# Values of a three-branch attention layer: turned on TensorE, or by VectorE's 32x32 turns and a trip through DRAM

## What is computed

```python
h = rmsnorm(x, norm_w[layer])
proj = h @ w_in[layer]
# 8 stick-breaking heads, each block of 128 queries against the keys up to its end
z = einsum('bhqd,bhkd->bhqk', qb, kb) * scale
log_fail = where(strict, -softplus(z), 0.0)
a = where(strict, exp(log_sigmoid(z) + suffix_sum(log_fail)), 0.0)
outs.append(einsum('bhqk,bhkd->bhqd', a, vb))
# 8 forgetting heads: causal softmax of q.k/8 + cum[t] - cum[s], then the same product with vb
# 4 memory heads: softmax over 256 memory tokens
y = rmsnorm_per_head(concat(sb_out, fx_out, m_out)) * out_norm_w * silu(gate)
x = x + y @ w_out[layer]
return rmsnorm(x, final_norm_w)
```

## Time and profile before

| | |
|---|---|
| median of 3 runs | 793.46 us (793.13 to 793.98) |
| the profiled execution: its own time | 793.03 us |
| its span, first to last instruction | 791.1 us |
| mean granted TensorE clock | 0.998 of full speed |
| busy: PE, DVE, ACT, POOL | 776.6, 605.0, 445.7, 257.7 us |
| DMA | 37708 packets, 93.25 MB, mean 118 GB/s |

### The profile page before, as it was taken

How to read it: one execution, slowest core, us unless ns; L and a number is a source line. 1 busy time by engine, 2 the same in 40 slices (tenths; PEclk the granted TensorE clock), 3 DMA queues, 4 the chain that set the end, 5 groups by cost and what they waited for, 6 DMA issues and landing times.

```text
span 791.1 us, 11916 instructions
## 1 busy us (share of the span) xinstructions
PE 776.6 (98%) x4030; PEld 653.2 (83%) x4030; DVE 605.0 (76%) x1206; ACT 445.7 (56%) x920; POOL 257.7 (33%) x440
## 2 busy tenths in 40 slices
PE   8999999999999999999999999999999999999997
PEld 8878887888888888888888888888888887878775
DVE  6877687776789777768977777898767688685676
ACT  7767765556646555665745667465555574542232
POOL 1112733242156326223823521383234124210000
PEclk9999999999999999999999999999999999999999
DMA  9413824124113412521261142106213398233523
GB/s 355 134 63 141 278 98 148 54 69 106 67 54 98 144 40 69 134 67 54 65 175 41 68 125 77 54 27 178 76 55 81 110 386 300 82 107 107 187 96 143
DMA packets 37708, 93.25 MB, mean 118 GB/s; under 512 B 5000, under 2 KB 13192, under 8 KB 36624
## 3 DMA queue, kind: packets, MB, share of 16 engines
q1 hardware_dynamic: 37648, 92.50, 36.1%
HBM read 61.91 MB, written 21.66 MB: 106 GB/s over the span
## 4 chain that ended last, share of the span: by engine, by line
PE 85%; DVE 7%; DMA 2%; ACT 2%; issue 2%; SPq 0%; POOL 0%; ACTq 0%; DVEq 0%; POOLq 0%
PE banks L867 16%; PE banks L869 15%; PE banks L868 15%; PE banks L1037 8%; PE banks L912 8%; PE banks L1057 5%; PE banks L1024 4%; PE banks L1056 4%; PE banks L1023 4%; PE banks L1108 1%; DMA hT<-wo_dram 1%; PE banks L984 1%; DMA work<-part_dram 1%; PE banks L1077 1%; DVE pT L1876 1%
## 5 line engine op out<-in xcount | busy, mean ns | idle before, releaser
L867 PE MATMUL banks<-hT,w_parts 128*128 128x512 f32 x576 | 237.6, 412 | 0.3 <-DVE sb_heads L1735 0.2
L869 PE MATMUL banks<-hT,w_parts 128*128 128x512 f32 x576 | 225.8, 392 | 0.0
L868 PE MATMUL banks<-hT,w_parts 128*128 128x512 f32 x576 | 225.4, 391 | 0.0
L1266 ACT ACTIVATE pT<-banks 128x512 fp32r<-128x512 f32 x208 | 92.4, 497 | 126.7 <-PE banks L1037 126.4
L1876 DVE TENSOR_TENSOR pT<-banks,pT 128x512 fp32r<-128x512 f32 x208 | 108.4, 563 | 66.6 <-ACT pT L1266 65.3
L869 PEld LDWEIGHTS banks<-hT,w_parts 128*128 128x128 f32 x576 | 108.1, 188 | 24.5
L867 PEld LDWEIGHTS banks<-hT,w_parts 128*128 128x128 f32 x576 | 108.5, 188 | 15.8 <-DVE sb_heads L1735 1.0
L868 PEld LDWEIGHTS banks<-hT,w_parts 128*128 128x128 f32 x576 | 109.0, 189 | 13.6
L1534 POOL TENSOR_TENSOR w_parts<-w_raw,w_parts 128x1024 fp32r<-128x1024 f32 x34 | 81.4, 2395 | 91.9 <-ACT w_parts L1165 91.9
L1541 POOL TENSOR_SCALAR_AFFINE_SELECT work<-work 128x128 f32<-128x128 f32 x64 | 30.4, 475 | 192.7 <-ACT work L1243 192.7
L1836 DVE TENSOR_TENSOR_SCAN work<-work 128x639 f32<-128x639 f32 (+3 forms) x64 | 90.7, 1418 | 0.7 <-POOL work L1541 0.6
(11 more groups left out here) (258 smaller groups left out, 1355.9 us busy)
## 6 DMA issues: line engine op xcount, KB each, us to landing
w_raw<-in_w_tiles SPq DMA_DIRECT2D x36, 512.0 KB, 3.9
hT<-wo_dram SPq DMA_DIRECT2D x14, 512.0 KB, 8.4
fx_heads<-fx_heads SPq DMA_DIRECT2D x8, 512.0 KB, 7.8
negL<-negL_dram SPq DMA_DIRECT2D x8, 512.0 KB, 6.1
yT_dram<-silu SPq DMA_DIRECT2D x8, 512.0 KB, 4.1
sb_heads<-sb_heads SPq DMA_DIRECT2D x8, 512.0 KB, 6.7
negL<-yT_dram SPq DMA_DIRECT2D x8, 512.0 KB, 4.9
work<-in_x SPq DMA_DIRECT2D x6, 512.0 KB, 6.7
```

The source lines that it names most:

```text
L867: pe.matmul(o, w[0][:, k, :], hT[:, 0, k, tok], start=(k == 0), stop=False)
L868: pe.matmul(o, w[0][:, k, :], hT[:, 1, k, tok], start=False, stop=False)
L869: mm = pe.matmul(o, w[1][:, k, :], hT[:, 0, k, tok], start=False, stop=(k == KT - 1))
L1266: act.activation(pT[:, n % 3, 0, cols], banks[:, T_BANK + n % 2, cols], ACT.Copy).then_inc(t_hi, 1)
```

## The change

The piece of values leaves PSUM by DVE's transpose, which turns each 32x32 block in place and writes it to the same buffer as the copy did. SP stores the buffer with four DMAs to a DRAM tensor in which the blocks stand at their turned places, and fetches it with one DMA, positions on the partitions, into the lower part's place of the value region. ACT copies from there to the upper part, DVE subtracts in place. The small job VT with its PE transposes and its use of the shared bank is gone; its semaphores `vt_hi` and `small_done` are replaced for the values by `v_out`, `v_in`, `v_hi`, `v_done`. The ticks of fetch and split come from a new table: for phases 3 to 9 the split is in ticks 13 and 15 of the phase before (c = 0, 1), for phase 2 in ticks 21 and 25. The load of the forget gates of the second head follows the fetch.

```diff
+def values_ticks():
+
+    out = []
+    for of in range(2, N_PH):
+        for c in range(2):
+            done = READ_TICK[piece_of("V", c, of)] - 1
+            fetch = max(done + 2, UNITS * (of - 1) + 7) if of > 2 else done + 8
+            out.append((of, c, fetch, max(fetch + 3, UNITS * (of - 1) + 13 + 2 * c) if of > 2 else fetch + 3))
+    return out
...
+    v_dram = nc.dram_tensor("v_dram", (N_PH, 2, CW, P), F32, kind="Internal").ap()
...
+        def v_in_rows(of, c):
+
+            return v_of(region_of(of))[:, 4 * c:4 * c + 4, 1:3, :]
...
+                if p.what == "V":
+                    store_values(q)
                 if closes_tile(p) and p.what == "K":
                     copy_keys(p.of, q)
 
+            def store_values(q):
+
+                p = PIECE[q]
+                sp.wait_ge(piece_done, q + 1)
+                rows = v_dram[p.of, p.c, :, :].rearrange("(j k) (i d) -> i k j d", k=Q4, d=Q4)
+                for i in range(P // Q4):
+                    sp.dma_start(rows[i], v_raw(p.of, p.c)[i * Q4:(i + 1) * Q4, :].rearrange("k (j d) -> k j d", d=Q4)).then_inc(v_out[p.c], 16)
+
+            def fetch_values(of, c):
+
+                sp.wait_ge(v_out[c], 64 * (of - 1))
+                if of > 2:
+                    sp.wait_ge(pv_done, STEP0[4 * (of - 1)])
+                else:
+                    for j in (1, 2):
+                        sp.wait_ge(wo_out[j], 32)
+                sp.dma_start(v_in_rows(of, c).bitcast(F32).rearrange("p b x c -> p b (x c)"),
+                             v_dram[of, c, :, :].rearrange("(b p) w -> p b w", p=P)).then_inc(v_in[c], 16)
+                if c == 1 and PHASES[of][0] == "fx":
+                    load_negL(PHASES[of][1], 1)
...
                 for q in DONE[i]:
                     piece_end(q)
+                for of, c, fetch, _ in VALUES:
+                    if i == fetch:
+                        fetch_values(of, c)
...
-                if p.what == "VT":
-                    pe.wait_ge(piece_done, piece_of("V", p.c, p.of) + 1)
-                    for b in range(4):
-                        mm = pe.transpose(o[:, b * P:(b + 1) * P], v_raw(p.of, p.c)[:, b * P:(b + 1) * P], ident[:, :])
...
                 if t.first and t.group % 4 == 0 and x0.kind != "mm":
-                    pe.wait_ge(small_done, small_of("VT", 1, x0.ph) + 1)
+                    pe.wait_ge(v_done, 2 * (x0.ph - 1))
...
+            def values_hi(of, c):
+                act.wait_ge(v_in[c], 16 * (of - 1))
+                act.activation(v_of(region_of(of))[:, 4 * c:4 * c + 4, 0::3, :], v_in_rows(of, c).bitcast(F32), ACT.Copy).then_inc(v_hi, 1)
...
                 if u % UNITS < 2:
 
-                    act.wait_ge(small_ready, READY_BEFORE[small_of("VT", 1, t.ph)] + 1)
+                    for c in range(2):
+                        act.wait_ge(v_out[c], 64 * (t.ph - 1))
...
-                    dve.tensor_copy(v_raw(p.of, p.c), src).then_inc(piece_done, 1)
+                    dve.transpose(v_raw(p.of, p.c), src).then_inc(piece_done, 1)
...
-                elif p.what == "VT":
-                    dve.wait_ge(vt_hi, VT_BEFORE[n] + 1)
-                    d = v_of(region_of(p.of))[:, 4 * p.c:4 * p.c + 4, :, :]
-                    dve.tensor_tensor(d[:, :, 1:3, :], src.rearrange("p (b h c) -> p b h c", b=4, h=2),
-                                      d[:, :, 0::3, :].bitcast(F32), ALU.subtract).then_inc(small_done, 1)
...
+            def values_lo(of, c):
+                dve.wait_ge(v_hi, 2 * (of - 2) + c + 1)
+                v = v_of(region_of(of))[:, 4 * c:4 * c + 4, :, :]
+                dve.tensor_tensor(v[:, :, 1:3, :], v[:, :, 1:3, :].bitcast(F32), v[:, :, 0::3, :].bitcast(F32), ALU.subtract).then_inc(v_done, 1)
```

More of the change, by code:

```diff
@@ L290, in small_pieces @@
             out.append(Small("N3", c, ph - 1, UNITS * ph + N3_AT + N3_LATER.get(ph - 1, 0)))
[L291 to L299, removed]
     for c in (1, 0):
@@ L307 @@
 SMALL_AT = [[n for n, p in enumerate(SMALL) if p.tick == i] for i in range(N_TICKS)]
-READY_BEFORE = firsts(1 if p.what in ("VT", "MT", "NT") else 0 for p in SMALL)
+READY_BEFORE = firsts(1 if p.what in ("MT", "NT") else 0 for p in SMALL)
 NT_BEFORE = firsts(1 if p.what == "NT" else 0 for p in SMALL)
-VT_BEFORE = firsts(1 if p.what in ("VT", "MT") else 0 for p in SMALL)
+MT_BEFORE = firsts(1 if p.what == "MT" else 0 for p in SMALL)
+def values_ticks():
[6 more added lines that the diff above has]
+    return out
+VALUES = values_ticks()
 def next_phase(i, at, later={}):
@@ L977, in small @@
                 p = SMALL[n]
-                if n and p.what in ("VT", "MT", "NT"):
+                if n and p.what in ("MT", "NT"):
                     pe.wait_ge(small_done, n)
                 o = banks[:, SMALL_BANK, :]
-                if p.what == "VT":
-                    pe.wait_ge(piece_done, piece_of("V", p.c, p.of) + 1)
-                    for b in range(4):
-                        mm = pe.transpose(o[:, b * P:(b + 1) * P], v_raw(p.of, p.c)[:, b * P:(b + 1) * P], ident[:, :])
-                elif p.what == "MT":
+                if p.what == "MT":
                     pe.wait_ge(piece_done, piece_of("memV", p.c, None) + 1)
@@ L1207, in split_next, with mem_values_hi @@
                     split_hi(w_follows(PIECE[q].tile))
-            def values_hi(n):
+            def mem_values_hi(n):
                 p = SMALL[n]
                 act.wait_ge(small_ready, READY_BEFORE[n] + 1)
[L1212 to L1224, removed]
+                for b in range(MB):
+                    ins = act.activation(mem_v[:, b, p.c, 0::3, :],
+                                         banks[:, SMALL_BANK, b * P:(b + 1) * P].rearrange("p (h c) -> p h c", h=2), ACT.Copy)
+                ins.then_inc(mt_hi, 1)
+            def values_hi(of, c):
+                act.wait_ge(v_in[c], 16 * (of - 1))
+                act.activation(v_of(region_of(of))[:, 4 * c:4 * c + 4, 0::3, :], v_in_rows(of, c).bitcast(F32), ACT.Copy).then_inc(v_hi, 1)
             def sigmoids(u):
@@ L1442, in _ @@
             for n in range(len(MEM_VALUES_AT)):
-                values_hi(n)
+                mem_values_hi(n)
             evacuate(7)
@@ L1490, in _ @@
                 for n in SMALL_AT[i]:
-                    if SMALL[n].what in ("VT", "MT"):
-                        values_hi(n)
+                    if SMALL[n].what == "MT":
+                        mem_values_hi(n)
                     if SMALL[n].what == "N1" and SMALL[n].of == LAST:
@@ L1496, in _ @@
                         y_end_hi(SMALL[n].of - LAST + 1, SMALL[n].c)
+                for of, c, _, at in VALUES:
+                    if i == at:
+                        values_hi(of, c)
                 for n in SMALL_AT[i + 1] if i + 1 < N_UNITS else []:
@@ L1764, in finish_small @@
                 if p.what == "MT":
-                    dve.wait_ge(vt_hi, VT_BEFORE[n] + 1)
+                    dve.wait_ge(mt_hi, MT_BEFORE[n] + 1)
                     for b in range(MB):
@@ L2082, in _ @@
                     lower_part(n)
+                for of, c, _, at in VALUES:
+                    if i == at:
+                        values_lo(of, c)
                 for n in SMALL_AT[i]:
```

7 lines of the change are left out of this document (2 added, 5 removed).

## The result

Slower by 1%: 801.23 us against 793.72 us for the kernel before on the same chip, ratio 1.010 (95% interval 1.0087 to 1.0112). I had forecast 787.9 us, in a range of 785.6 to 790.9. The profiled execution took 803.15 us (span 801.2), 1.9 us above the median of its runs; against the 793.03 us of the profiled execution before (span 791.1) that is 10.1 us more.

What follows compares the result with a forecast made beforehand. PE's own instruction stream was taken to set the pace nearly everywhere. A PE gain of 6.9 us less 1.3 us of border stalls, other terms 0, gave 5.6 us: from 793.46 to 787.9 us, range 785.6 to 790.9.

Steps and rivals of the forecast that it cites:

- PE's gain: On TensorE: removing four transposes saves 0.43 us per piece of values, 6.9 us for 16 pieces.
- The recorded duration: Rival on PE: each transpose is worth its 272 ns duration, so the time falls to 776 us; chance 0.02.
- The border stalls: Moved copy and subtract delay PE's scores into phases 4 and 6 (0.4 us each) and 9 (0.5): 1.3 us lost.
- The landing: Each piece's stores of 128 B runs to DRAM land after about 8 us, hidden, so costing 0.
- 512 B rule: Trainium skill's rule against small DMA runs: 512 B for full rate, read-modify-write below; kept as a rival.
- factor of 19: Skill's warning on turning by strided plain copy: a 3.9 us landing would become 74, and the time exceed about 945 us.
- DMAs and SP's queue: Four added stores and one fetch per piece, 80 issues on SP, stay hidden before the next weight load: 0 us.
- The stores hold SP: Rival: 40 us landings hold SP's queue, weight loads come 22 us late in seven phases, about 945 us; chance 0.04.
- The subtract waits for POOL: Rival: DVE's subtract waits out POOL's split at seven borders, 12 us less the 6.9 gained: 798.5 us; chance 0.07.

Runs made afterwards that it cites:

- the version with the borders moved: Changed kernel with phase 2's splits at ticks 28 and 36, later phases' splits at 13 and 14 (stick-breaking running) or 12 and 14 (forgetting): 789.39 us, ratio 0.9942.
- the late splits: Changed kernel with phase 2's two splits (ACT's copy, DVE's subtract) at ticks 28 and 36 instead of 21 and 25: 788.93 us, ratio 0.9946 to the kernel before.
- the long-run experiment: Changed kernel with values stored as rows of 2048 B instead of 128 B runs, leaving them in wrong places: 801.46 us, ratio 1.0098 to the kernel before.
- the two profiles: Changed kernel profiled at 803.15 us, then run again unchanged for a second profile; that run took 801.77 us.

## Why the prediction was wrong

The sign was wrong through one step. By the others:

- **PE's gain: right.** 0.43 us a turn from the starts; 0.43 by the ticks (6.1 us for 14 pieces, about 0.8 for the other two). By the Trainium skill ("TensorE: Matmul & The Clock Gate", Part 4), whose figure is for bf16, it would have been 0.275 us for each transpose; four of them gave 0.43, 0.11 each. The recorded duration (272 ns) agrees with the page and is not a price on a full PE.
- **The border stalls: right** in place and size at three (0.4, 0.4, 0.5 us), and undone one by one in the version with the borders moved. Smaller losses of 0.1 to 0.3 us at ticks 49, 92 and 124 I had not counted. With the late splits the whole came to 4.7 us less than before, where my sum was 5.6.
- **The landing: wrong and harmless.** I scaled 3.9 us by the number of runs to 8; it is 2.6 to 3.2. The Trainium skill's 512 B rule ("DMA: Bandwidth & Descriptors", Specifications) agrees in direction with the 0.5 to 0.6 us a store of the long-run experiment. Its factor of 19 ("VectorE: DVE Perf Modes", The three transpose paths) compares with the hardware's DMA transpose, which no run here used; no store of the changed kernel came near the 74 us that I had worked out from it (the longest landed after 5.2).
- **"DMAs and SP's queue": the step that failed.** It ended "At 8 us after about 241 they land near 249, before the next weight load is due at 250.8. So I take 0." Phase 3 stood for all phases, and what I asked was whether the new stores would delay SP's old work. The harm went the other way: SP's old work delayed the new fetch. For phases 3 to 9 the fetches are ordered at tick 7 or 8 of the phase before, six to eight ticks ahead of the copy; for phase 2 at ticks 18 and 22, three ahead, on a queue that is busy with w_out until 104 and then stands for POOL until 123.9 (119.5 in the kernel before, where it could be read). I wrote "(for phase 2: 21 and 25)" and never held these ticks against the earlier trace rows's counterpart in phase 1. The term was 0 and should have been 13 to 14 us: 9.0 to 10.6 in the two stops at the scores, the rest the reduced clock and slowed work around them.
- **The rivals.** My slower ones had the right parts of the machine and the wrong places. "The stores hold SP" blamed the landing. "The subtract waits for POOL" was priced at the borders, at 1.7 us each, where the subtract met only the last 0.17 us of POOL's split and took 0.72 us; but the mechanism, read off, is real, as three versions showed when the subtract met nearly a whole split. "The stores hold SP" also gave 945 us without taking off the 6.9 us of gain, which the sum for POOL does; it changes nothing.

So the sum of the two profiles is: phase 1 +14.0 and +13.1, borders and small losses after it +2.8 in both, turns -6.9, which gives +9.9 and +9.0 where their ends stand at +10.2 and +8.9. Both executions lay above the median (by 1.9 and 0.5 us), by which the excess is 7.5 us.

## What to carry to other kernels

When a change puts a transfer in a value's path, follow the new transfer itself through its queue in every phase, the first ones above all: ask what stands ahead of it there and which engine that waits for, before asking what it delays. A steady phase proves nothing for the phases that are ordered by other rules. And when a loss sits in one place, move the consumer before giving up the change: here two tick numbers turned +7.5 us into -4.7.

## What the runs showed of the hardware

- A PE stop can cost more than its length. After the 7.2 us stop the granted clock was 0.50 for 5 us, about 2.2 us lost on top. After a first stop of 2.2 to 2.7 us three profiles show 0.53 to 0.61 from 112 to 115 us, 1.5 to 1.7 us lost; after the 3.4 us stop of the changed kernel's first profile the clock stayed at 1.00 from 109 to 118. What decides it I can't tell from these runs.
- A DVE subtract with both inputs in SBUF takes 0.68 us alone and took 2.49 and 2.85 us beside POOL's 2.4 us split. It waited the split out and did not share with it: in all 19 places in these traces where it starts while the split runs, it ends 0.55 us after the split, whether they overlap by 0.17 us (it takes 0.72) or by 2.3 (2.85). The scale step of the earlier trace rows was the hint.
- A 16 KB store issued just behind loads of 256 and 512 KB landed after 4.7 to 5.3 us (four profiles), without them just ahead after 2.2 to 2.4 (three). A small transfer that others wait for is better issued ahead of large ones; here PE's stop at tick 33 was 0.4, 0.8 and 1.1 us with both late splits and the loads ahead, and 0.4 in all three with the fetch moved.
- A store of 64 KB in 128 B runs lands in 2.6 to 3.2 us (median); with runs of 2048 B in 2.1 to 2.6.
